# Modulation of layer 0 as unsplit fp32 matmuls on four column tiles, with a ring of its own

## What is computed

```python
def ada_params(cond, w, b):
    mod = jax.nn.silu(cond) @ w + b
    return jnp.split(mod, 3, axis=-1)
...
sh_c, sc_c, g_c = ada_params(c_ctx, ada_w[layer], ada_b[layer])
xm_l = x_lat * (1.0 + sc_l) + sh_l
xm_c = x_ctx * (1.0 + sc_c) + sh_c
```

## Time and profile before

| | |
|---|---|
| median of three timed runs | 3155.72 us (3155.25 to 3158.48) |
| span of the profiled execution, first to last instruction | 3157.5 us |
| that execution's own time | not listed apart; the three timed runs lie 2.3 us under to 1.0 us over its span |
| PE busy / mean granted clock | 98 % / 0.994 |
| first stage, `mem_k` | 0 to 195.8 us, 6 % of the span |

### The profile page before, as it was taken

How to read it: one execution, slowest core, us unless ns; L and a number is a source line. 1 busy time by engine, 2 the same in 40 slices (tenths; PEclk the granted TensorE clock), 3 DMA queues, 4 the chain that set the end, 5 groups by cost and what they waited for, 6 DMA issues and landing times.

```text
span 3157.5 us, 45097 instructions
## 1 busy us (share of the span) xinstructions
PE 3086.2 (98%) x16842; PEld 2654.5 (84%) x16842; DVE 2218.5 (70%) x2768; ACT 1640.1 (52%) x2000; POOL 53.6 (2%) x52
## 2 busy tenths in 40 slices
PE   7999999999999999999999999999999999999998
PEld 6788878888788887888888888888888888888887
DVE  7779877788677777656757855567456777777544
ACT  6665444546534566544556655445345555555443
POOL 0011300000000000000000000000000000000000
PEclk9999999999999999999999999999999999999999
DMA  8978675787568765655555565566345555555554
GB/s 297 351 249 287 239 276 201 282 323 237 176 221 282 254 203 181 206 173 189 172 188 172 168 199 187 189 226 197 135 150 184 187 186 186 187 191 194 189 190 139
DMA packets 180248, 666.42 MB, mean 211 GB/s; under 512 B 20084, under 2 KB 20468, under 8 KB 178808
## 3 DMA queue, kind: packets, MB, share of 16 engines
q1 hardware_dynamic: 178424, 660.09, 61.7%
q10 hardware_dynamic: 1664, 4.19, 0.3%
HBM read 657.91 MB, written 6.29 MB: 210 GB/s over the span
## 4 chain that ended last, share of the span: by engine, by line
PE 85%; DVE 7%; DMA 4%; ACT 2%; DVEq 1%; issue 1%; ACTq 0%; SPq 0%
PE acc L762 45%; PE acc L766 22%; PE acc L773 4%; PE acc L775 4%; PE acc L774 4%; DVE w_lo L1990 3%; DMA ada_raw<-in_w_ada 2%; ACT w_hi L1277 1%; DMA mod_raw<-in_w_mod 1%; DVE mod_raw L2001 1%; PE acc L930 1%; DMA raw<-in_w_mix_out 0%; PE msc L1172 0%; PE msc L876 0%; PE msc L1192 0%
## 5 line engine op out<-in xcount | busy, mean ns | idle before, releaser
L1990 DVE TENSOR_TENSOR w_lo<-raw,w_hi 128x1024 fp32r<-128x1024 f32 x1020 | 1242.3, 1227 | 564.1 <-ACT w_hi L1277 554.6
L1277 ACT CAST w_hi<-raw 128x1024 fp32r<-128x1024 f32 x1020 | 1061.8, 1049 | 805.6 <-PE acc L766 571.3
L762 PE MATMUL acc<-a_pair,w_hi 128*128 128x512 f32 x2944 | 931.6, 398 | 4.6 <-DVE a_pair L2905 2.4
L766 PEld LDWEIGHTS acc<-a_pair,w_lo 128*128 128x128 f32 x2944 | 554.1, 188 | 131.1
L766 PE MATMUL acc<-a_pair,w_lo 128*128 128x256 f32 x2944 | 579.3, 278 | 0.0
L762 PE MATMUL acc<-b_pair,w_hi 128*128 128x512 f32 x1792 | 569.4, 399 | 5.3 <-DVE w_lo L1990 5.2
L762 PEld LDWEIGHTS acc<-a_pair,w_hi 128*128 128x128 f32 x2944 | 451.2, 189 | 7.6 <-DVE a_pair L2905 2.8
L762 PE MATMUL acc<-f_pair,w_hi 128*128 128x512 f32 x1408 | 442.4, 395 | 0.0
L766 PEld LDWEIGHTS acc<-b_pair,w_lo 128*128 128x128 f32 x1792 | 337.5, 188 | 79.8
L766 PE MATMUL acc<-b_pair,w_lo 128*128 128x256 f32 x1792 | 353.0, 278 | 0.0
L766 PEld LDWEIGHTS acc<-f_pair,w_lo 128*128 128x128 f32 x1408 | 264.5, 188 | 62.5
(11 more groups left out here) (364 smaller groups left out, 2749.5 us busy)
## 6 DMA issues: line engine op xcount, KB each, us to landing
raw<-in_w_ffn_up SPq DMA_DIRECT2D x176, 512.0 KB, 3.9
mod_raw<-in_w_mod SPq DMA_DIRECT2D x128, 512.0 KB, 5.2
raw<-in_w_ffn_down SPq DMA_DIRECT2D x88, 512.0 KB, 3.3
ada_raw<-in_w_ada SPq DMA_DIRECT2D x64, 512.0 KB, 5.5
raw<-in_w_xa_k SPq DMA_DIRECT2D x32, 512.0 KB, 6.1
raw<-in_w_k SPq DMA_DIRECT2D x32, 512.0 KB, 4.6
raw<-in_w_v SPq DMA_DIRECT2D x32, 512.0 KB, 4.8
raw<-in_w_even_out SPq DMA_DIRECT2D x32, 512.0 KB, 4.6
```

Of the source, the lines that this page charges most:

```text
L762: pe.matmul(acc[:, bank(stage, g) + m, :], w_h[:, cols], pair[:, :, kc, :], start=begin, stop=False, skip_group_check=True)
L766: mm = pe.matmul(acc[:, bank(stage, g) + m, 0:T], w_l[:, cols], pair[:, 0, kc, :], start=False, stop=end, skip_group_check=True)
L1277: nc.scalar.copy(w_hi[:, slot], source).then_inc(hi_done, 1)
L1990: vec.tensor_tensor(w_lo[:, slot], source, w_hi[:, slot].bitcast(F32), ALU.subtract).then_inc(lo_done, 1)
```

## The change

- `ada_raw` gets twelve places instead of four: four where it was, eight (`ada_more`) in the space of `a_pair`, which is unused until the context is modulated. The keys, which share `w_hi` and `w_lo` with the a units before, have the split rings to themselves.
- Modulation units are no longer split: no cast on ACT, no subtraction on DVE. PE multiplies the landed fp32 data directly, with a stationary operand `cond_tile` of 32 columns (two used).
- Four groups of output columns are taken together as a "quad": for each of two chunks, four matmuls write to PSUM partitions 0, 32, 64 and 96, one column tile each, of one bank. Sixteen quads, two rounds of eight.
- Key units become the only units of `mem_k` (32). Quads stand in the side function, one ahead of each of 16 of the units 1 to 21. SP issues key j+2 ahead of the quad of unit j; a quad's place is free when PE has used it (`ada_used`), not when DVE has split it.
- The memory's pair (`b_pair`) is made ahead of the first split; the memory is loaded ahead of any weight.
- Per round ACT copies a whole 128 x 512 bank and PE makes four 128 x 128 transposes; `make_mod` reads those with four additions.

```diff
-ADA_FIRST = 6
-ADA_RING = 4
+ADA_TILES = 4
+ADA_ROUNDS = ADA_GROUPS // ADA_TILES
+ADA_RING = 12
 ADA_OVER = 22
...
+ADA_QUADS = ADA_UNITS // ADA_TILES
+QUADS = ADA_QUADS // ADA_ROUNDS
+ADA_AT = {j: range(j * ADA_QUADS // ADA_OVER, (j + 1) * ADA_QUADS // ADA_OVER) for j in range(ADA_OVER)}
+ADA_LAST = [next(j for j in ADA_AT if QUADS * (r + 1) - 1 in ADA_AT[j]) for r in range(ADA_ROUNDS)]
+KEYS_AHEAD = 2
...
+                def load_quad(quad):
+                    first, k = divmod(quad, QUADS)
+                    for tile in range(ADA_TILES):
+                        n = ADA_TILES * quad + tile
+                        if n >= ADA_RING and tile == 0:
+
+                            sp.wait_ge(ada_used, (n - ADA_RING) // ADA_TILES + 1)
+                        nc.sync.dma_start(ada_slot(n).rearrange("p a b -> p (a b)"),
+                                          t["w_ada"][(ADA_TILES * first + tile) * QUADS + k]).then_inc(ada_landed[n % ADA_RING], 16)
+
+                load_mem()
+                load_key(0)
+                load_constants()
+                for j in range(1, stage.n):
+                    load_key(j)
+                    for quad in ADA_AT.get(j - KEYS_AHEAD, ()):
+                        load_quad(quad)
...
-                            pe.wait_ge(lo_done, i * stage.n + (u + 1 + RING))
-                            for c in range(KU):
-                                kc = KU * k + c
-                                pe.matmul(msc[:, ada_bank, :], cond_pair[:, kc, :], w_hi[:, slot, c, :],
-                                          start=(first and c == 0), stop=False)
-                                mm = pe.matmul(msc[:, ada_bank, :], cond_pair[:, kc, :], w_lo[:, slot, c, :],
-                                               start=False, stop=(last and c == KU - 1))
-                            mm.then_inc(unit_used, 1)
...
+                for n in range(ADA_TILES * quad, ADA_TILES * (quad + 1)):
+                    pe.wait_ge(ada_landed[n % ADA_RING], 16 * (n // ADA_RING + 1))
+                for c in range(KU):
+                    for tile in range(ADA_TILES):
+                        rows = slice(tile * (P // ADA_TILES), (tile + 1) * (P // ADA_TILES))
+                        mm = pe.matmul(msc[rows, 1 + first, :], cond_tile[:, KU * k + c, :], ada_slot(ADA_TILES * quad + tile)[:, c, :],
+                                       start=(k == 0 and c == 0), stop=(k == QUADS - 1 and c == KU - 1))
+                mm.then_inc(ada_used, 1)
...
-                    for c in range(32):
-                        mm = pe.transpose(msc[:, 0, 4 * c:4 * c + 4], mod_rows[:, c * P:(c + 1) * P], ident[0:4, 0:4])
...
+                    for c in range(NCOL // P):
+                        mm = pe.transpose(msc[:, 3 if n == 0 else 1, c * P:(c + 1) * P], mod_rows[:, n, c * P:(c + 1) * P], ident[:])
```

More of the change, by code:

```diff
@@ L99, in __init__ @@
             groups, group_units = 2 * groups, group_units // 2
-        self.group_units, self.groups, self.ada, self.gate = group_units, groups, ada, gate
+        self.group_units, self.groups, self.gate = group_units, groups, gate
         self.n_w = groups * group_units
         self.kinds = [("w", *divmod(n, group_units), (n + 1) % group_units == 0) for n in range(self.n_w)]
[L104 to L112, removed]
         if gate:
@@ L122 @@
 STAGES = [
-    Stage("mem_k", "w_xa_k", "F", 1, groups=4, ada=(0, ADA_UNITS), dve=1),
+    Stage("mem_k", "w_xa_k", "F", 1, groups=4, dve=1),
     Stage("ctx_k", "w_k", "F", 1, gate=True, act=1, dve=1),
@@ L189, in ring_place @@
 def ring_place(stage, j):
-    return PLACE["w"].index((stage.name, j)) if stage.ada else stage.u0 + j - ADA_UNITS
+    return stage.u0 + j
 def spread(n, k):
@@ L209 @@
 LAM_AT = 8
[L210 to L213, removed]
+CTX_LOAD_AT = 21
+MEM_SUM_AT = 2
+MEM_ROOT_AT, MEM_SCALE_AT, MEM_TURN_AT, MEM_TAKE_AT = 3, 3, 6, 8
+MOD_ROWS_AT = {max(_j, 1): _r for _r, _j in enumerate(ADA_LAST)}
+MOD_SUM_AT = {min(_j + 2, CTX_AT - 2): _r for _j, _r in MOD_ROWS_AT.items()}
 TURN_KEYS_AT = (6, 8)
@@ L219 @@
 STATES_AT = 9
-assert all(kind[0] == "w" for kind in STAGE["mem_k"].kinds[MOD_TURN - 1:])
+assert max(MOD_ROWS_AT) < MOD_TURN
 KV_GROUP = {"mem_k": 0, "mem_va": 4, "mem_vb": 5}
@@ L404, in build @@
         mem = wk("mem", [P, DC, T], 32 * K)
-        ada_raw = wk("ada_raw", [P, ADA_RING, KU, NCOL], 48 * K)
-        cond_pair = wk("cond_pair", [P, DC, P], 80 * K, F32R)
+        ada_raw = wk("ada_raw", [P, 4, KU, NCOL], 48 * K)
+        ada_more = place("ada_more", [P, 8, KU, NCOL], F32, a_pair_at)
+        cond_tile = wk("cond_tile", [P, DC, P // ADA_TILES], 80 * K)
         kv_stage = wk("kv_stage", [P, 2, 2 * NCOL], 72 * K)
         cond = wk("cond", [P, DC, 2], 64 * K)
-        cond_silu = wk("cond_silu", [P, DC, 2], 64 * K + 128)
         rows = wk("rows", [4, 16, T], 0)
@@ L563, in both_sides, with ada_slot @@
             return side
+        def ada_slot(n):
+            return ada_raw[:, n % ADA_RING] if n % ADA_RING < 4 else ada_more[:, n % ADA_RING - 4]
         def used(stage):
@@ L596, in load_first, with load_key @@
             def load_first(stage):
-                for j, (kind, g, k, _) in enumerate(stage.kinds):
-                    if stage.name == "mem_k" and j == ADA_RING:
-                        load_mem()
+                def load_key(j):
+                    g, k = stage.kinds[j][1:3]
                     if j == CTX_LOAD_AT:
@@ L604, in load_first @@
                         nc.sync.dma_start(x[:], t["ctx"]).then_inc(ctx_in, 16)
[L605 to L614, removed]
+                    if j >= RING:
+                        sp.wait_ge(lo_done, j + 1)
+                    nc.sync.dma_start(raw[:, j % RING].rearrange("p a b -> p (a b)"),
+                                      t[stage.weights][stage.group_units * g + k]).then_inc(raw_landed[j % RING], 16)
+                def load_quad(quad):
[13 more added lines that the diff above has]
+                        load_quad(quad)
             def load(stage):
@@ L678, in _ @@
                     nc.sync.dma_start(decay[:], t["decay"]).then_inc(ret_in, 16)
-                if stage.ada:
+                if stage is STAGES[0]:
                     load_first(stage)
@@ L798, in two_chunks, with modulation @@
                 return msc[:, first + c // 2, (c % 2) * T + tt * P:(c % 2) * T + (tt + 1) * P]
-            steps.wait(dve=2)
+            steps.wait(dve=1)
             steps.end("cond")
             steps.end("mem_pair")
-            def mem_sums(j):
[L807 to L816, removed]
+            def modulation(quad):
+                first, k = divmod(quad, QUADS)
+                if quad == 0:
+                    pe.wait_ge(act_step, AFTER["cond"]["act"])
+                for n in range(ADA_TILES * quad, ADA_TILES * (quad + 1)):
[6 more added lines that the diff above has]
+                mm.then_inc(ada_used, 1)
+            def mem_sums(j):
+                for quad in ADA_AT.get(j, ()):
+                    modulation(quad)
+                if j == MEM_SUM_AT:
+                    pe.wait_ge(consts_in, 48)
+                    for q in range(4):
+                        steps.wait(act=q + 1)
+                        for c in range(4 * q, 4 * q + 4):
+                            mm = pe.matmul(msc[:, 0, 0:T], ones[:], x[:, c, :], start=(c == 0), stop=(c == DC - 1))
+                    steps.done(mm)
                 if j == MEM_TURN_AT:
@@ L1315, in finish @@
                     return whole if (g % 2 or by_half) and group else None
-                walk_stage(act, stage, split, {"w": finish, "a": rows_out, "x": forget_exp}, side,
+                walk_stage(act, stage, split, {"w": finish, "x": forget_exp}, side,
                            (done, stage.act), (dve, stage.dve))
@@ L1399, in _, with mem_squares @@
             act.wait_ge(cond_in, 16)
-            steps.done(nc.scalar.activation(cond_silu[:], cond[:], ACT.Silu))
-            act.drain()
             steps.wait(dve=1)
-            steps.done(nc.scalar.copy(cond_pair[:, :, 0:4:2], cond_silu[:]))
+            steps.done(nc.scalar.activation(cond_tile[:, :, 0:2], cond[:], ACT.Silu))
             steps.end("cond")
+            def mem_squares(q):
+                steps.done(nc.scalar.activation(x[:, 4 * q:4 * q + 4, :].rearrange("p a b -> p (a b)"),
+                                                mem[:, 4 * q:4 * q + 4, :].rearrange("p a b -> p (a b)"), ACT.Square))
+            act.wait_ge(params_in, 16)
+            for q in range(4):
+                act.wait_ge(mem_in[q], 16)
+                for c in range(4 * q, 4 * q + 4):
+                    mm = nc.scalar.activation(b_hi[:, c, :], mem[:, c, :], ACT.Copy, scale=col("norm_mem", c))
+                steps.done(mm)
+            steps.end("mem_pair")
             for j in range(RING):
                 split(STAGES[0], 0, j)
+                if j >= 1:
+                    mem_squares(j - 1)
             def mem_chunks(j):
```

(36 more changed lines are left out.)

51 lines of the change are left out of this document (17 added, 34 removed).

## The result

| | before | after |
|---|---|---|
| median, timed side by side | 3157.1 us (3155.25 to 3160.63, four runs) | 3129.02 us (3126.19 to 3131.09, four runs) |
| span of the profiled execution | 3157.5 us | 3127.3 us |
| next stage's first `a_pair` matmul | 195.76 us | 165.19 us |

The ratio is 0.9908, 95 % interval 0.9894 to 0.9922: 28 us faster, where 20 were forecast. In the profiled executions the first stage ends 30.6 us earlier and the span is 30.2 us shorter, so what the stage gained arrives at the end.

What follows compares the result with a forecast made beforehand. A cycle of load, cast, subtract and free place bound `mem_k`; afterwards transfers would, landing last at 141.4 us. With the tail the stage ends at 175.7 against 195.76: 3155.72 - 20 = 3136 us, range 3125 to 3160.

Steps and rivals of the forecast that it cites:

- The mechanism: In `mem_k`, load, cast, subtraction and late-freed ring places bound the stage at 322 GB/s; afterwards transfers set the pace.
- I take 370: Transfer rate in GB/s assumed for `mem_k` with a full queue: 50.9 MB, last landing at 141.4 us.
- The limit of 358 GB/s: HBM limit per core from the skill, weighed but not used: landing at 146 us, end about 5 us later.
- The tail: `mem_k` after the last landing: last quad, eleven key units, four transposes; 33.4 to 35.1 us, stage end about 175.7 us.
- four at a time: Case where a quad's matmuls overlap on all four column tiles: 1.73 us a quad, PE's sum before the last quad 108 us.
- PE's terms: PE's work in `mem_k` before the last quad: 108 or 134 us, both under 141.4, so hidden by transfers.
- The start: Beginning of `mem_k`: parameters and memory land, the memory's pair is made, one subtraction; 15.1 us.
- two at a time: Case where program order lets only two of a quad's matmuls overlap: 3.46 us a quad, PE's sum 134 us; called likelier.
- A price for the changes of tiling mode: Engine drains at 32 changes between quads and full-width matmuls: 0 to 13 us, hidden or up to 6 us late.
- The clock: PE's granted clock in `mem_k`: mostly 2.4 GHz, half-speed start +5.6 us inside the 141, tail 0 to +4, taken as 0.
- Serial tiles: Rival: column tiles in `mem_k` do not overlap, 6.92 us a quad, PE bound, 224 us, about 3186 us; chance 0.13.
- No change at 322 GB/s: Rival: the full queue in `mem_k` still averages this rate, or overlap is about 1.35; 3150 to 3162 us; chance 0.09.

Runs made afterwards that it cites:

- the ring alone: Kernel before with twelve instead of four places for modulation units, splits and full-width matmuls kept: 3146.5 us (median of six runs), ratio 0.9962.
- the run on one tile: Changed kernel with all quads but the first of each round sending their matmuls to one column tile instead of four: 3188.06 us (one run).

## Why the prediction was right, and where its size was off

**The mechanism held.** "A cycle of load, cast, subtract and free place" bound the stage: the ring alone gives 12.0 us. The evidence I took from the earlier trace rows was weaker than I thought: in that run SP's waits still add up to 112.6 us, and the stage is shorter all the same. The better evidence was the swinging rate in the earlier trace rows.

**The step that was mis-sized is "I take 370".** The queue moved 409 GB/s. I divided the rate of a stage that ran empty by turns by its share (353/0.95), but rate per share is not constant: 219/0.62 = 353, 392/1.00 = 392, and now 409/1.03 = 397. The nearest row was the one at full share, 392. A second term partly offset it: by 132.11 us 128.31 us x 409 GB/s = 52.5 MB had moved, not 50.9, since keys issued ahead of need and the first stores were on the way too. 50.9 MB at 370 are 137.6 us, 52.5 at 409 are 128.3: 9.3 us, and the last quad starts at 132.11, not 141.4. Of the 10.5 us that the forecast of the stage's end (175.7) was late, this is nearly all; the remaining 1.2 us are the tail, 33.1 us where the middle of its bounds was 34.3. The limit of 358 GB/s that I weighed from the Trainium skill was further off. The same page of the Trainium skill, "DMA: Bandwidth & Descriptors", in section "iDMA fabric — 4 AXI ports for 8 engines, asymmetric across TPBs", gives 408.7 GB/s for one core's load stream issued from SP with the neighbour idle, and the trace agrees (409).

**The tail** came out as worked for four at a time: 165.19 - 132.11 = 33.1 us, against 33.4.

**PE's terms** were hidden, as the sum said. The start was 16.07 us (15.1). A quad took 1.92 us, four at a time (bound 1.73); "two at a time", which I had called the likelier, did not hold. It cost the forecast about 0.9 us, since I took the middle between the two. A price for the changes of tiling mode barely shows: the first pair of full-width matmuls after a quad spans 0.74 us, where the others span 0.63:

```profile
132.11 1.92 PE L810 MATMUL msc<-ada_raw,cond_tile 128*32 128x512 f32 x16 [1.24 <-DMA ada_raw<-in_w_ada]
133.97 0.74 PE L756 MATMUL acc<-b_pair,w_hi 128*128 128x512 f32 x2
```

**The clock**, taken as 0 to +4 us on the tail and set to 0: the row 140 to 160 us shows 1.00. It fell once, to 0.91 and 0.92, around the pause of 6.06 us ahead of the quad at 119.33, which then took 3.64 us. I had expected pauses of 2 to 3 us each; the other seven were 0.3 to 1.7 us, and that one stands behind the 2 MB of context, which I had counted in the bytes but not seen as a pause.

**The rivals.** Serial tiles: refuted by the quads, and its price confirmed by the run on one tile. No change at 322 GB/s: refuted by the rate. The point that I gave for it, an overlap of about 1.35, was far off; the overlap is 7.05/1.92 = 3.7.

## What to carry to other kernels

Where both PE and the DMA engines seem partly idle and the rate swings from stretch to stretch, look for a ring whose places come free late; then ask what becomes the bound next, since here the deeper ring alone stopped at 12 of 31 us, and the cheaper matmuls alone, without the ring, lost 35 (there one quad took all the places). A rate for a full queue is read from the rows at full share, not scaled up from rows at a lower one; here even the row at full share, 392, was 4 % under what the full queue moved. A large transfer that is needed late does not belong ahead of small ones that the critical path awaits.

## What was not expected of the hardware

An issue of 512 KB on SP took 0.33 us right after a pause of SP, and about 1.07 us later, in a stretch of unbroken issues with the DMA engines at full share (timeline of SP in the changed kernel):

```profile
15.96 0.33 SPq L609 DMA_DIRECT2D raw<-in_w_xa_k  x1
...
46.38 0.33 SPq L609 DMA_DIRECT2D raw<-in_w_xa_k  x1
...
94.08 1.07 SPq L609 DMA_DIRECT2D raw<-in_w_xa_k  x1
95.19 4.44 SPq L619 DMA_DIRECT2D ada_more<-in_w_ada  x4
99.67 1.89 SPq L609 DMA_DIRECT2D raw<-in_w_xa_k  x1
```

The short issue at 46.38 us stands in a stretch whose share is 1.03 too, behind a pause of SP, so the share alone does not make an issue long. The median way from issue to landing was 14.6 us for `ada_more` and 13.2 for the keys, against 5.5 for `ada_raw` and 6.1 for the keys before (part 6 of both pages). I read the long issue as the sign of a full queue, which would make pieces of SP in the chain transfers in another guise; no run was made to test that. It is not likely that the issues themselves set the pace: four of them take 4.48 us from 95.19 to 99.67, which is an estimated 468 GB/s for 2.1 MB, more than the 409 that moved. The mean share of the DMA engines reads up to 1.03, so 1.00 was not the ceiling of that column.
